# Projection matmuls ahead of the scores in the even units of a stick-breaking attention step

## The reference, cut to what matters

```
q, k, v, xq = split_cols(h @ w_in, [D_MODEL, D_MODEL, D_MODEL, X_WIDTH])
z = einsum('bhqd,bhkd->bhqk', qi, k) * SCALE
past = kpos[None, :] < tpos[:, None]
log_fail = where(past, log_sigmoid(-z), 0.0)
after = cumsum(log_fail, axis=3, reverse=True) - log_fail
a = where(past, exp(log_sigmoid(z) + after), 0.0)
o = einsum('bhqk,bhkd->bhqd', a, v)
```

## Time and profile before

| | |
|---|---|
| median of 3 runs | 1505.14 us (1505.09 to 1507.27) |
| the profiled execution, its own time | 1497.31 us |
| its span, first to last instruction | 1495.5 us |
| mean granted TensorE clock | 0.979 of full |
| TensorE matmuls busy | 1427.9 us, 95% |
| VectorE busy | 863.6 us, 58% |
| ScalarE busy | 555.0 us, 37% |
| steps 0 to 6 of the attention | about 168 to 605 us |
| step 7 | about 605 to 678 us |

### The profile page before, as it was taken

How to read it: one execution, slowest core, us unless ns; L and a number is a source line. 1 busy time by engine, 2 the same in 40 slices (tenths; PEclk the granted TensorE clock), 3 DMA queues, 4 the chain that set the end, 5 groups by cost and what they waited for, 6 DMA issues and landing times.

```text
span 1495.5 us, 19880 instructions
## 1 busy us (share of the span) xinstructions
PE 1427.9 (95%) x7212; PEld 1170.6 (78%) x7212; DVE 863.6 (58%) x1294; ACT 555.0 (37%) x939; POOL 30.0 (2%) x29
## 2 busy tenths in 40 slices
PE   6988999999999999599999999999999999999998
PEld 4766787787877878477877888888888888888887
DVE  5556788898888988875243353442525334252535
ACT  6445556565565655643242212121211212121110
POOL 0000000000000000510000000000000000000000
PEclk8999899999999999699999999999999999999999
DMA  6100001000000010114011221110211111021102
GB/s 211 43 17 13 28 22 30 21 28 28 21 28 21 28 29 13 58 57 141 1 57 38 71 61 39 46 56 28 70 42 56 42 42 56 28 70 43 57 15 113
DMA packets 92610, 69.91 MB, mean 47 GB/s; under 512 B 7312, under 2 KB 78992, under 8 KB 92560
## 3 DMA queue, kind: packets, MB, share of 16 engines
q1 hardware_dynamic: 92560, 69.24, 15.0%
HBM read 65.03 MB, written 4.19 MB: 46 GB/s over the span
## 4 chain that ended last, share of the span: by engine, by line
PE 88%; DVE 5%; ACT 2%; issue 2%; DMA 1%; SPq 1%; POOL 0%; DVEq 0%; ACTq 0%
PE ps L974 32%; PE ps L1025 16%; PE ps L283 15%; PE ps L877 6%; PE ps L337 5%; PE ps L321 4%; PE ps L311 3%; PE ps L254 2%; PE ps L696 1%; PE ps L234 1%; DVE hl L678 1%; PE ps L836 1%; DVE v_s L467 1%; PE ps L667 1%; DMA mw_raw<-in_w_mem_kv 1%
## 5 line engine op out<-in xcount | busy, mean ns | idle before, releaser
L974 PE MATMUL ps<-f_h,gw_h 128*128 128x512 f32 x704 | 274.7, 390 | 4.2 <-issue 4.2
L974 PE MATMUL ps<-f_h,gw_l 128*128 128x512 f32 x704 | 274.0, 389 | 0.0
L974 PE MATMUL ps<-f_l,gw_h 128*128 128x512 f32 x704 | 274.0, 389 | 0.0
L1041 DVE TENSOR_TENSOR x<-ps,x 128x512 f32<-128x512 f32 x176 | 121.5, 691 | 81.5 <-PE ps L1025 77.6
L974 PEld LDWEIGHTS ps<-f_h,gw_h 128*128 128x128 f32 x704 | 132.2, 188 | 31.9 <-issue 4.8
L974 PEld LDWEIGHTS ps<-f_h,gw_l 128*128 128x128 f32 x704 | 132.1, 188 | 27.6
L974 PEld LDWEIGHTS ps<-f_l,gw_h 128*128 128x128 f32 x704 | 132.2, 188 | 27.1
L406 ACT ACTIVATE a_h<-ps 128x256 fp32r<-128x256 f32 (+2 forms) x96 | 78.0, 812 | 185.6 <-PE ps L321 185.6
L283 PE MATMUL ps<-hh,w_h 128*128 128x512 f32 x336 | 141.0, 420 | 0.0
L1025 PE MATMUL ps<-dw_h,gu_h 128*128 128x512 f32 x352 | 137.0, 389 | 0.0
L1025 PE MATMUL ps<-dw_l,gu_h 128*128 128x512 f32 x352 | 137.0, 389 | 0.0
(11 more groups left out here) (173 smaller groups left out, 2357.6 us busy)
## 6 DMA issues: line engine op xcount, KB each, us to landing
w_raw<-in_sb_w_in SPq DMA_DIRECT2D x52, 256.0 KB, 2.9
f_raw<-in_w_gate SPq DMA_DIRECT2D x44, 256.0 KB, 3.0
f_raw<-in_w_up SPq DMA_DIRECT2D x44, 256.0 KB, 3.0
f_raw<-in_w_down SPq DMA_DIRECT2D x44, 256.0 KB, 2.7
wo_raw<-in_w_out SPq DMA_DIRECT2D x20, 256.0 KB, 2.8
x_in<-in_x SPq DMA_DIRECT2D x8, 512.0 KB, 8.8
out<-x SPq DMA_DIRECT2D x8, 512.0 KB, 2.6
mw_raw<-in_w_mem_kv SPq DMA_DIRECT2D x4, 512.0 KB, 8.9
```

Source lines behind the costliest of these rows:

```text
L974: mm = pe.matmul(ps[:, 4 + 2 * fb + mat], w[:, fb, mat, k], f[half][:, k], start=(k == 0 and i == 0), stop=(k == KC - 1 and i == 2))
L1041: dve.tensor_tensor(o, ps[:, (2, 3, 0, 1)[d % 4]], o, ALU.add).then_inc(s_x2, 1)
```

## The change

In the step's loop over units, the block of the part (or, in step 7, of the piece of the output projection) moves from behind the scores to ahead of them. At odd u there are no scores, so nothing moves there. In unit 0 the order goes from scores, part, transposes to part, scores, transposes; in units 2, 4, 6, 8 and 10 from transposes, scores, part to transposes, part, scores. In step 7 the same holds for units 6 and 8, the two in which both a piece and scores stand. No instruction is added or removed, and no other engine's order changes.

```diff
             for u in range(NU):
                 if u:
                     pe_transposes(pe, s, u)
+                if not last:
+                    pe_part(pe, s + 1, 1 - par, u // 2, 4 * (u % 2))
+                elif u >= FILL_AT:
+                    pe_project(pe, u - FILL_AT)
                 if u % 2 == 0:
                     for ahead in (u + 2, u + 3):
                         if ahead < NU:
                             pe_scores(pe, s, ahead, par)
                         elif not last:
                             pe_scores(pe, s + 1, ahead - NU, 1 - par)
-                if not last:
-                    pe_part(pe, s + 1, 1 - par, u // 2, 4 * (u % 2))
-                elif u >= FILL_AT:
-                    pe_project(pe, u - FILL_AT)
                 if u == 0:
                     pe_transposes(pe, s, u)
                 if u % 2:
```

## The result

The changed kernel took **1523.76 us** in the median of 4 executions (1521.39 to 1526.54), the kernel before 1505.12 (1500.49 to 1507.27). The two medians are 18.6 us apart; the ratio is 1.0132, with a 95% interval of 1.0113 to 1.0150, which would be 19.9 us. The forecast was 1520 within 1511 to 1530.

What follows compares the result with a forecast made beforehand. TensorE's matmuls were taken to bound the kernel, so only new waits cost: 1.9 us a step, seven times 13.3, plus 1.5 in step 7, makes 14.8; added to 1505.14 this gave 1520 us, range 1511 to 1530.

Steps and rivals of the forecast that it cites:

- TensorE sets the pace, and only waits can cost: Steps with a projection: TensorE busy 60.45 of 62.44 us; its matmul sum is unchanged, the change can only make it wait.
- Units 4 to 7, 1.3 a step: Late scores of 6 delay fail, scans, low part of 5 and weights; TensorE waits, transposes of 7 come 1.3 us later.
- Units 7 to 9, 0.5: Late fail of 10 delays values of 9, 0.3 us; unit 7 and the wait before unit 8's part, together 0.2.
- the lateness feeds on itself: Rival, 12%: VectorE never catches up, units 4, 6 and 8 each lose 1.3 to 1.9; 4.5 us a step, 1538.
- Unit 2, 0.1; units 0 and 10 nothing: Unit 2 has six transposes in place of eight, 0.1 us; boundary waits or distant use cover units 0 and 10.
- Seams, taken as 0 within ±1.0: TensorE's changeovers between transposes, scores and part in six units: -1.0 to +1.0 us a step, taken as 0.
- Step 7, 1.5: Unit 6: scores of 8 and 9 come behind the wait for the first add, uncovered, 1.5 us; range 1 to 4.
- The sum: Whole kernel: seven steps' 13.3 us plus step 7's 1.5 make 14.8 us slower.
- The clock: Rival, 3%: new waits make the clock fall once a step, adding 1.4 us in each of seven steps; 1530.
- The cover holds: Rival, 7%: ScalarE's 24.0 us of waits for transposes take up the lateness, only step 7 pays; 1506.6.
- faster: Rival, 4%: seams save 0.2 us in five units of seven steps, 7 us, with no new wait; 1499.6.

Runs made afterwards that it cites:

- Unit 4 alone: Kernel before, with the part ahead of the scores only in unit 4 of steps 0 to 6; 63.80 us a step, +1.34.
- unit 6 alone: Kernel before, with the part ahead of the scores only in unit 6 of steps 0 to 6; 62.69 us a step, +0.23.
- unit 8 alone: Kernel before, with the part ahead of the scores only in unit 8 of steps 0 to 6; 62.98 us a step, +0.53.
- the kernel with units 0, 2 and 10: Kernel before, with the part ahead of the scores only in those units of steps 0 to 6; 1506.88 us beside 1501.18.
- e6_low_half_first: Changed kernel, with VectorE taking the projected half's low part ahead of the unit's first scan; 1532.16 us, 65.92 a step at full clock.
- e7_weight_tile_later: Changed kernel, with ScalarE making unit 4's weight tile in unit 5, behind the high part of 5; 1521.28 us, 65.07 a step at full clock.

## Why the prediction came out as it did

- *TensorE sets the pace, and only waits can cost.* Held. Busy times of the other engines didn't move, and steps without new waits kept their length to 0.1.
- *Units 4 to 7, 1.3 a step.* The mechanism held link by link: counted from the transposes of 4, fail is 2.42 late (2.35 forecast), then scans, low part, weights, and a wait for the low part of k of 0.93 from start to start (0.95). Measured 1.5 to 1.6 in place. Two small errors: the values of 5 waited 0.50 from start to start where I had next to nothing, and took another 0.2 behind it; the wait of 0.45 for the weights of 6 was not there as a wait, since the values had taken it. Unit 4 alone costs 1.34, with unit 6 in its old order; the part that then comes early adds 0.3 between 6 and 7, not 0.9, because without it the same lateness is met by the transposes of 7.
- *Units 7 to 9, 0.5.* **The mis-sized term.** From the transposes of 7 to those of 10 the whole change loses 0.94 in the step shown and 0.98 in the mean, twice the forecast. It is not carried over from units 4 to 7: unit 6 alone loses 0.30 in unit 7, where I thought fail of 8 well covered, and unit 8 alone 0.51 in units 8 and 9, where I had 0.3 (the values of 9 wait 0.46 there). Together these are 0.81 of the 0.98. What units add to each other, 0.4 a step between 6 and 7, was in my chain for units 4 to 7. My rival "the lateness feeds on itself" (4.5 a step) did not come about: behind the transposes of 9 the whole change loses 0.60 and unit 8 alone 0.56, so the lateness does not grow from unit to unit.
- *Unit 2, 0.1; units 0 and 10 nothing.* Held: 0.07 between the transposes of 2 and 4 in the whole change, nothing at the boundary and behind unit 10, though the wait for v is 0.7 in place of 0.50 (its seams save as much).
- *Seams, taken as 0 within ±1.0.* Right for this change, whose seams are as many. That they are not free was shown only when a kernel had more of them: 0.26 a block.
- *Step 7, 1.5.* 1.6, alone as in company.
- *The sum.* 13.3 + 1.5 forecast; 18.2 + 1.6 measured. Of the 4.9 that the steps cost more than forecast, some 3.4 are the term for units 7 to 9 (0.98 in place of 0.5 a step) and 1.8 that for units 4 to 7 (1.56 in place of 1.3); all else came to 0.05 in place of 0.1. From median to median the kernel became 18.6 slower, where 14.8 were forecast.
- *The clock.* In the changed kernel's profile it stayed at 1.00 through the steps. As a mechanism the rival exists: three kernels of this study had steps at 1.5 more by it. By rows it doesn't take a new wait: in the kernel with units 0, 2 and 10 it fell behind the boundary's old ones, 0.75 in place of 0.50 and 1.01 as before.
- *The cover holds, or faster.* ScalarE's cover was used up in part: in one step its waits for transposes fell from 21.3 (the 24.0 of the earlier trace rows has a boundary more) to 10.2. VectorE's scans of 6 had no such cover, they started right behind fail in the kernel before.

## What to carry to other kernels

When two pieces of work change places on the engine that sets the pace, its own sum says nothing. Follow the result of the piece that is now later through every queue to the point where it is needed, and compare the delay with the idle time that stands in front of the consumer in that very unit, not with the engine's idle share. Charge a wait only once: where a nearly full engine is late (VectorE is busy 86% of the step), removing the wait you see moves it to its next product. The cheap gain is often an in-order engine standing at one item with ready work behind it: here swapping VectorE's items at the boundary, and putting independent matmuls between an item and its round trip, took 1.1% off.

## What the runs showed of the hardware

- A block of scores on half of the array's rows between full-array matmuls costs 0.26 us in seams on the mean; the rows of one show 0.09 at its entry, 0.12 behind its first pair and 0.10 at its exit.
- The clock at a boundary falls or not in the same kernel with the same waits (0.75 and 1.01, with the two transposes of unit 0 between them): it fell in three of six steps of the kernel with units 0, 2 and 10, and, behind waits of 0.7 to 0.8 and 1.0, in three of six of e6_low_half_first, one of six of e7_weight_tile_later and none of six with the whole change. The granted clock of the first 4 us behind such a fall is 0.60 on the mean, part of it at the lower level of 1.2 GHz, and a fall costs 1.5 us. I had taken from the kernel before that rests of this size are safe; they are not. The Trainium skill (TensorE: Matmul & The Clock Gate, "HAM oscillation — how this bites in real kernels") warns of pauses between bursts of matmuls, in an example with far longer pauses; these runs show such a fall behind pauses of 0.75 and 1.01 us.
- The values of 5 behind a wait of 0.33 took 1.06 us as a group in place of 0.86. This is no rule for a wait: the values of 9, behind 0.35 to 0.49 in the six steps, took 1.86 to 1.92, before 1.80 to 1.92.
